# A second buffer for hT, finer waits of the gather, later constants and norm rows, and the wide expert one quad earlier

## What is computed

```python
def grouped_moe(x, router_w, router_b, w_gate, w_up, w_down):
    scores = jax.nn.sigmoid((t @ router_w).astype(jnp.float32))
    ...   # best of 4 groups, the top 2 experts in it, weights normalised
    for e in range(N_EXPERTS):                      # 16
        h = jax.nn.silu(t @ w_gate[e]) * (t @ w_up[e])      # 2048 -> 512
        y = y + combine[:, e:e + 1] * (h @ w_down[e])       # 512 -> 2048
    return y.reshape(B, S, D)
# in each layer
x = layer_norm(ALPHA * x + mix, ln_mix_g[i], ln_mix_b[i])
ffn = grouped_moe(x, ...)
x = layer_norm(ALPHA * x + ffn, ln_ffn_g[i], ln_ffn_b[i])
```

## Time and profile before

| | us |
|---|---|
| median of 3 runs (lowest, highest) | 1734.02 (1733.76, 1738.78) |
| the profiled execution's own time | 1737.14 |
| its span, first to last instruction | 1735.3 |
| mean granted clock of TensorE | 0.960 |

### The profile page before, as it was taken

The page is one execution under the profiler, slowest core; times in us unless marked ns, Lnnn a source line. Parts: engine busy times, 40 slices in busy tenths (PEclk is TensorE's granted clock), DMA queues, the critical chain, the costliest instruction groups (busy, mean ns, idle before and its releaser), DMA issues.

```text
span 1735.3 us, 19026 instructions
## 1 busy us (share of the span) xinstructions
PE 1585.9 (91%) x7841; PEld 934.2 (54%) x7841; DVE 668.1 (39%) x937; ACT 432.7 (25%) x551; POOL 29.4 (2%) x26
## 2 busy tenths in 40 slices
PE   6999999988989999999869999997999999999993
PEld 5888786875344343343338878785434334334331
DVE  4445335535123231323265474455232222222226
ACT  4334335324110111010135353333111110101112
POOL 1000000000000000000022000000000000000000
PEclk9999999997999999999979999898999999999997
DMA  9554323555999999999966565345799997998993
GB/s 364 205 194 191 122 97 128 212 182 207 420 427 414 428 427 428 428 428 428 428 261 251 189 224 182 131 165 224 282 428 428 427 428 308 422 375 361 429 427 142
DMA packets 47316, 531.18 MB, mean 306 GB/s; under 512 B 5361, under 2 KB 5905, under 8 KB 7938
## 3 DMA queue, kind: packets, MB, share of 16 engines
q1 hardware_dynamic: 45234, 518.08, 73.4%
q0 software_dynamic: 2000, 11.95, 1.9%
HBM read 527.91 MB, written 2.10 MB: 305 GB/s over the span
## 4 chain that ended last, share of the span: by engine, by line
PE 85%; DVE 6%; DMA 3%; ACT 3%; issue 1%; SPq 0%; POOL 0%; DVEq 0%; ACTq 0%
PE bank L1023 37%; PE bank L689 10%; PE bank L690 10%; PE bank L691 10%; PE bank L991 4%; PE bank L1072 4%; DMA w_all<-in_moe_w_down 3%; PE bank L1055 2%; PE bank L823 2%; ACT y_hi L1490 1%; PE bank L1002 1%; DVE X L2094 1%; PE bank L1110 1%; PE bank L896 1%; DMA w_land<-in_ev_w_in 1%
## 5 line engine op out<-in xcount | busy, mean ns | idle before, releaser
L1023 PE MATMUL bank<-w_all,xg 128*64 128x512 f32 x2048 | 454.5, 596 | 1.6 <-DVE hT L2074 1.4
L689 PE MATMUL bank<-w_hi,T_hi 128*128 128x512 f32 x768 | 303.1, 395 | 7.1 <-DVE w_lo L1650 4.6
L690 PE MATMUL bank<-w_lo,T_hi 128*128 128x512 f32 x768 | 301.0, 392 | 0.0
L691 PE MATMUL bank<-w_hi,T_lo 128*128 128x512 f32 x768 | 300.6, 391 | 0.0
L1650 DVE TENSOR_TENSOR w_lo<-w_land,w_hi 128x2048 fp32r<-128x2048 f32 (+1 forms) x96 | 214.2, 2240 | 210.7 <-ACT w_hi L1295 210.6
L1023 PEld LDWEIGHTS bank<-w_all,xg 128*64 128x64 f32 x2048 | 140.9, 137 | 278.3 <-issue 274.3
L1295 ACT CAST w_hi<-w_land 128x2048 fp32r<-128x2048 f32 (+1 forms) x100 | 184.3, 1854 | 247.9 <-PE bank L691 237.0
L1023 PE MATMUL bank<-w_all,hT 128*64 128x512 f32 x992 | 227.6, 602 | 2.2 <-DMA w_all<-in_moe_w_down 2.2
L2094 DVE SCALAR_TENSOR_TENSOR X<-bank,weight,X 128x512 f32<-128x512 f32 x256 | 174.4, 744 | 69.0 <-PE bank L1072 68.9
L2083 DVE TENSOR_TENSOR y_lo<-bank,y_hi 128x512 fp32r<-128x512 f32 x62 | 42.6, 688 | 387.3 <-ACT y_hi L1490 387.3
L689 PEld LDWEIGHTS bank<-w_hi,T_hi 128*128 128x128 f32 x768 | 145.4, 189 | 38.7 <-issue 3.1
(11 more groups left out here) (282 smaller groups left out, 1037.9 us busy)
## 6 DMA issues: line engine op xcount, KB each, us to landing
w_all<-in_moe_w_gate_up SPq DMA_DIRECT2D x128, 2048.0 KB, 15.1
w_all<-in_moe_w_down SPq DMA_DIRECT2D x64, 2048.0 KB, 18.9
w_land<-in_ev_w_in SPq DMA_DIRECT2D x32, 1024.0 KB, 4.8
w_land<-in_od_w_in SPq DMA_DIRECT2D x32, 1024.0 KB, 4.8
w_land<-in_ev_w_out SPq DMA_DIRECT2D x16, 1024.0 KB, 4.8
w_land<-in_od_w_out SPq DMA_DIRECT2D x16, 1024.0 KB, 4.8
w_land<-in_att_w SPq DMA_DIRECT2D x7, 1024.0 KB, 4.7
x0T<-in_xT SPq DMA_DIRECT2D x4, 512.0 KB, 9.7
```

Source lines behind the costliest of these rows:

```text
L689: pe.matmul(dst, hi_l, hi_r, start=start, stop=False)
L690: pe.matmul(dst, hi_l, lo_r, start=False, stop=False)
L691: return pe.matmul(dst, lo_l, hi_r, start=False, stop=stop)
L1023: ins = pe.matmul(dst[halves[h], :], cols(c), U.weights(q, pos + h)[:, c, :], start=start and c == 0, stop=stop and c == 3)
```

## The change

- hT has two buffers, hT_even and hT_odd, by the expert's number; product(e) waits only for the y_hi of expert e-2.
- The gather's wait for y_lo is taken apart: none before the first fill, half 0 before the second (bank 2), half 1 before the third (bank 3). The same holds in gather_wide.
- SP issues const behind the first twelve loads; PE waits for it behind block 1 and ACT before its sine tables. DVE's waits for const and for the small constants, ahead of its preparation of the sine tables, stay where they are.
- POOL issues the six small constants and the first norm rows only once PE has used 16 units, which is the end of block 3.
- In the last quad scatter(2, 1) is done between the two groups of the last down, and DVE does y_lo(3, 0) ahead of add(2, 1).
- WIDE_Q is 1: the wide expert stands at place 4, the fifth, and gather_wide serves the second quad.

```diff
@@ -50,7 +50,7 @@
 ROUNDS = SEQ // CAP
-WIDE_Q = 2
+WIDE_Q = 1
 WIDE = 4 * WIDE_Q
@@ -331,7 +331,8 @@
         gsil = moe_buf("gsil", [P, 4, ALL])
-        hT = moe_buf("hT", [P, 4, ALL])
+        hT_even, hT_odd = moe_buf("hT_even", [P, 4, ALL]), moe_buf("hT_odd", [P, 4, CAP])
+        hT = (hT_even, hT_odd)
         xg_x = moe_buf("xg_x", [P, KT, MORE])
@@ -510,8 +511,6 @@
         def _(sp):
-            sp.dma_start(const[:], A["const"]).then_inc(ident_in, 16)
-
             def load(g, j, src, n=NB, ring=w_land):
@@ -521,6 +520,7 @@
                 load(1, j, unit(w_in0, 0, j))
+            sp.dma_start(const[:], A["const"]).then_inc(ident_in, 16)
             with sp.Fori(1, IN0_FULL // 2) as i:
@@ -635,6 +635,33 @@
         def _(pool):
+            def load_rows(g, b, n):
+
+                if n:
+                    pool.wait_ge(rows_used, n)
+                pool.dma_start(rows[:, 0, :], g.partition_broadcast(P)).then_inc(rows_in, 16)
+                pool.dma_start(rows[:, 1, :], b.partition_broadcast(P)).then_inc(rows_in, 16)
...
+            pool.wait_ge(t_low, 8)
+            pool.wait_ge(used, 16)
             for dst, src in ((rw[:], A["router_w"]),
...
                 pool.dma_start(dst, src, allow_slow_non_contiguous=True).then_inc(const_in, 16)
-
-            def load_rows(g, b, n):
...
-            pool.wait_ge(t_low, 8)
             load_rows(A["ln_mix_g"][0:1], A["ln_mix_b"][0:1], 0)
@@ -734,7 +734,6 @@
-            pe.wait_ge(ident_in, 16)
             for j in range(4):
@@ -745,6 +744,7 @@
+            pe.wait_ge(ident_in, 16)
             pe.wait_ge(gemm_out_a, 1)
@@ -978,9 +978,12 @@
-            def gather(Q, n, qs=range(8)):
+            def gather(Q, n, qs=range(8), down_rows=None):
+
...
                 for q in qs:
+                    if q in (1, 2) and down_rows is not None:
+                        pe.wait_ge(y_lo_done, down_rows + q - 1)
                     if q >= 3:
@@ -992,9 +995,11 @@
-            def gather_wide(Q):
+            def gather_wide(Q, down_rows):
...
                 for t in range(KT):
+                    if t in (1, 2):
+                        pe.wait_ge(y_lo_done, down_rows + t - 1)
                     if t >= 3:
@@ -1087,16 +1092,18 @@
-                    def down(pos, e, following):
+                    def down(pos, e, following, between=None):
...
                             ge(pe, y_lo_done, 2 * E + (0 if is_wide(layer, q, e - 1) else p - 1))
-                            two_units(pos + 2 * p, bank[2 + p], lambda c: hT[:, c, 0:CAP], True, True)
+                            two_units(pos + 2 * p, bank[2 + p], lambda c: hT[e % 2][:, c, 0:CAP], True, True)
                             if p == 0 and following is not None:
...
                                 slots(following)
+                            if p == 0 and between:
+                                between()
@@ -1107,7 +1114,7 @@
                                 for c in range(4):
-                                    ins = pe.matmul(bank[2 + h][0:ALL, :], hT[:, c, :], U.weights(q, pos + 2 * p + h)[:, c, :],
+                                    ins = pe.matmul(bank[2 + h][0:ALL, :], hT_even[:, c, :], U.weights(q, pos + 2 * p + h)[:, c, :],
                                                     start=c == 0, stop=c == 3)
@@ -1148,16 +1155,14 @@
                         pe.wait_ge(slots_out, 4 * Q + 4)
-                        pe.wait_ge(y_lo_done, 2 * (4 * Q + 2) + 2)
                         if is_wide(layer, q, 4):
                             pe.wait_ge(twice_ready, Q + 2)
-                            gather_wide(Q + 1)
+                            gather_wide(Q + 1, 2 * (4 * Q + 2) + 1)
                         else:
-                            gather(Q + 1, 4)
+                            gather(Q + 1, 4, down_rows=2 * (4 * Q + 2) + 1)
                     first_sums(2, 3)
                     if last:
-                        scatter(2, 1)
-                        down(48, 3, None)
+                        down(48, 3, None, lambda: scatter(2, 1))
                         first_sums(3, None)
...
@@ -1323,7 +1328,6 @@
-            act.wait_ge(ident_in, 16)
             for j in range(4):
@@ -1349,6 +1353,7 @@
                                    accum_out=att[:, 2 * w + a:2 * w + a + 1]).then_inc(rms_sq, 1)
+            act.wait_ge(ident_in, 16)
             act.wait_ge(trig_ready, 1)
@@ -2070,11 +2075,11 @@
                         dve.wait_ge(silu_done, E + 1)
-                        ge(dve, y_hi_done, 2 * E)
-                        ins = dve.tensor_tensor(hT[:, :, 0:CAP], gsil[:, :, 0:CAP],
+                        ge(dve, y_hi_done, 2 * (E - 1))
+                        ins = dve.tensor_tensor(hT[e % 2][:, :, 0:CAP], gsil[:, :, 0:CAP],
                                                 bank[7][:, 0:4 * CAP].rearrange("p (c s) -> p c s", c=4), ALU.mult)
                         if is_wide(layer, q, e):
-                            ins = dve.tensor_tensor(hT[:, :, CAP:ALL], gsil[:, :, CAP:ALL], bank[6][:, 4 * CAP:8 * CAP]
+                            ins = dve.tensor_tensor(hT_even[:, :, CAP:ALL], gsil[:, :, CAP:ALL], bank[6][:, 4 * CAP:8 * CAP]
                                                     .rearrange("p (c s) -> p c s", c=4)[:, :, MORE:2 * MORE], ALU.mult)
@@ -2138,8 +2143,9 @@
                     if last:
+                        y_out(3, 0)
                         add(2, 1)
-                        down(3, None)
+                        y_out(3, 1)
                         add(3, 0)
...
```

More of the change, by code:

```diff
@@ L637, in _ @@
         def _(pool):
[L638 to L644, removed]
             def load_rows(g, b, n):
@@ L671, in _ @@
             pool.wait_ge(t_low, 8)
+            pool.wait_ge(used, 16)
+            for dst, src in ((rw[:], A["router_w"]),
+                             (rbias[:], A["router_b"].rearrange("(o e) -> o e", o=1).partition_broadcast(P)),
+                             (gains[:, 0, :], A["ev_q_norm"][0].rearrange("(t p) -> p t", t=4)),
+                             (gains[:, 1, :], A["ev_kv_norm"][0].rearrange("(t p) -> p t", t=4)),
+                             (gnorm[:], A["ev_gla_norm"].partition_broadcast(P)),
+                             (posi[:], pos_v)):
+                pool.dma_start(dst, src, allow_slow_non_contiguous=True).then_inc(const_in, 16)
             load_rows(A["ln_mix_g"][0:1], A["ln_mix_b"][0:1], 0)
@@ L1212, in overflow @@
                         for p in range(2):
-                            two_units(4 + p, bank[2], lambda c: hT[:, c, 0:CAP], True, True)
+                            two_units(4 + p, bank[2], lambda c: hT_even[:, c, 0:CAP], True, True)
                             after(V_, OVER_DVE, ("y", p))
@@ L2168, in overflow @@
                         after(A_, OVER_ACT, "silu")
-                        dve.tensor_tensor(hT[:, :, 0:CAP], gsil[:, :, 0:CAP],
+                        dve.tensor_tensor(hT_even[:, :, 0:CAP], gsil[:, :, 0:CAP],
                                           bank[7][:, 0:4 * CAP].rearrange("p (c s) -> p c s", c=4), ALU.mult) \
```

## The result

| us | before | after |
|---|---|---|
| median (lowest to highest), 4 runs each | 1736.4 (1733.8 to 1740.3) | 1712.8 (1712.1 to 1715.6) |
| the profiled execution's span | 1735.3 | 1711.0 |
| mean granted clock of TensorE | 0.960 | 0.972 |
| start to the first expert group | 417.5 | 413.4 |
| first layer's experts, first group to end of last down group | 460.9 | 457.8 |

The ratio after to before is 0.9874, 95% interval 0.9852 to 0.9897. The median lies 2.6 us under the 1715.4 foretold, inside the forecast's own range. Before's four runs lie high: in the 15, 23 and 7 runs beside the experiments its median is 1734.3, 1734.0 and 1733.5, so the change is worth about 21 us rather than 23.6. The span is 24.3 us shorter: 4.1 in the start, 3.1 in the first layer's experts, 2.3 between, 14.7 in the second layer's.

What follows compares the result with a forecast made beforehand. It took PE and the expert weight stream to be balanced in the MoE stages, PE-bound elsewhere. Start 5.2, first layer -1.4, second layer 14.8 sum to 18.6 us off: 1715.4 us, own range 1711 to 1719.

Steps and rivals of the forecast that it cites:

- What bounds it: MoE stages: PE and the weight stream balanced, 29.1 against 29.5 us an expert; PE waits for weights from mid first layer.
- hT: Product before each scatter: second buffer saves PE 1.21 us an expert, 27.3 us in 22 waits; expert 24.8 us for 26.0.
- Gather: PE's wait for y_lo before a gather goes to nothing: 3.4 us plus 1.7 of low clock, about 5.1 a boundary.
- First layer: First layer's MoE stage: a loss of 1.4 us (bounds: gain 5.1 without the sharing, loss 2).
- They now share with loads 94 and 95: End of first MoE stage: norm rows, started about 2 us after issue, split engines with the last loads, costing 4.9 us.
- so I charge the low clock: Last down group of first layer: PE has idled about 4 us, so 1.7 us is added.
- Second layer: Second layer's MoE stage: a gain of 14.8 us (bounds 20.5 without sharing, 11 with a slower stream).
- rival 2: Start gives only 2 and second layer's stream loses 4 us more in hiccups: gain 11.4, 1722.5 us; chance 0.12.
- The move is almost free either way: Wide expert at fifth or ninth place in second layer: load 95 lands within 1 us either way.
- Start: Before the first full block: 2.96 small constants, 1.4 const, 0.8 spared low clock; 5.2 us (bounds 2.0 and 6.5).
- Rival 4: Weight-bound loads, about 58: new weight waits keep PE's clock low, 2.0 us each, 1831 us; chance 0.03.
- Rival 1: Ends of both MoE stages: norm rows don't delay the last loads; 31 us off, 1703 us; chance 0.15.

Runs made afterwards that it cites:

- experiment 1: Kernel before, with each pair load behind the first six of each MoE stage cut to 3072 of 4096 columns, overflow rounds never entered: 1730.0 us (0.9979).
- 2: Changed kernel, with each pair load behind the first six of each MoE stage cut to 3072 of 4096 columns, overflow rounds never entered: 1658.7 us (0.9562).
- 7: Changed kernel, with an expert's product waiting again for both y_hi copies of the expert before, as if hT were single: 1722.0 us (0.9932).
- 4: Changed kernel, with GpSimd issuing each MoE stage's norm rows only once PE has used load 94: 1707.6 us (0.9849).
- 9: Changed kernel, with PE waiting again for y_lo of both halves before the whole gather, also the wide one: 1715.8 us (0.9902).
- 3: Changed kernel, with the second layer's wide expert at the ninth place again (WIDE_Q = 2): 1711.6 us (0.9875).
- 8: Changed kernel, with norm rows issued after load 94 was used and the wide expert at the ninth place: 1706.5 us (0.9837).
- 5: Kernel before, with only GpSimd's small constants and first norm rows waiting for used 16, const still ahead of xT: 1732.4 us (0.9987).
- 6: Kernel before, with only const moved behind block 1's loads and PE's and ACT's waits for it moved along: 1734.2 us (0.9997).
- experiment 10: Changed kernel, with scatter(2, 1) ahead of the last expert's two down groups again: 1717.8 us (0.9912).

## Why the prediction was right, and where its steps were not

A number in brackets is that of an experiment.

- **What bounds it: right.** PE-bound before (experiment 1), balanced so closely that the stream took most of what PE gave (2). PE's first wait of some length for weights stands at load 34 of the first layer, a third into the stage and not in its middle:

```profile
565.85 1.51 PE L1028 MATMUL bank<-w_all,xg 128*64 128x512 f32 x6 [0.98 <-DMA w_all<-in_moe_w_gate_up]
```

- **hT: right.** 24.70 us an expert for 24.8 (2), the waits ahead of scatter gone, and its worth in the time 9 us for 27 of waits, or 12.6 once the rows are moved away (7, 4). The product behind the wide expert still makes PE wait for 1.40 us.
- **Gather: right in sum, wrong in the split.** The wait fell to nothing, but the finer waits by themselves carry 1 to 3 us of it (9); the early product carries the rest. The prediction had said so in a half sentence and still counted the 5.1 as one step.
- **First layer: wrong, -1.4 foretold, +3.1 found.** Two terms were mis-sized. "They now share with loads 94 and 95": the issue fell at 856.2, the packets flowed only from 860 (3.7 us behind it, where the prediction had about 2), so only load 95 paid, 2.5 us for the 4.9. And "so I charge the low clock": behind 2.59 us without matmuls the last group took 3.65 and the clock fell only at 876; 1.7 was charged for nothing. 2.4 and 1.7 are 4.1 of the 4.5 between foretold and found.
- **Second layer: 14.8 foretold, 14.7 found, with errors that cancel; that the sum came out is partly luck.** Load 40 was issued 185.1 us after the stage's first group, where the steps gave 1405.7 - 1221.9 = 183.8 (the clock was low for 6.9 us in the wide down groups, 1378.4 to 1385.3, where before had 3.4). From its landing (1404.9) to load 95's (1680.4) 275.5 us passed, 2.5 of them for the rows: 4.96 a load for 4.91, hence 2.9 us of hiccups more, rival 2's mechanism in part. Against these and the 1.3 stand 2.2 of the rows and 1.7 of the clock, as in the first layer.
- **"The move is almost free either way": nearly.** It costs 1.2 us by the medians and 3 by the stages (3, 8), where I had written within 1.
- **Start: 5.2 foretold, 3.8 to 4.1 found in the traces.** The medians of the two halves show less, 1.6 and nothing (5, 6), so the size is open. GpSimd's transfers 3.5 for 2.96, const 0.3 for 1.4, and the 0.8 of spared low clock did not come: the idle time ahead of the full block stayed (2.47 for 2.60).
- **Between the layers, a term I did not have: 2.3.** It is no effect of the change. The stretch of low clock near 1090 us differs from trace to trace. These windows are of before and of after, at the same place of the work:

```profile
1085.00:1102.00 17.00, 13.29 (x49) 10.59 (x48) 9.07 (x14) 5.02 (x7) 0.00 (x0) 0.70 0.21 80
```

```profile
1078.00:1095.00 17.00, 13.25 (x59) 10.56 (x58) 8.99 (x14) 4.92 (x7) 0.00 (x0) 0.90 0.21 79
```

Experiment 1, with the old program there, shows 341.0 us for this part, as after does, and experiment 6, with the old program too, 343.5.
- **Rival 4 (a low clock in the weight waits): out.** In 740 to 850 us, where PE waits 1.2 to 1.5 us for three loads in six, the granted clock is 1.00. The Trainium skill, "TensorE: Matmul & The Clock Gate", section "HAM oscillation — how this bites in real kernels", tells of longer waits for weights that lower the clock anew each time; waits as long as those did not arise here. Rival 1 was half true, as the rows cost 2.5.

## What to carry to other kernels

Where an engine and a stream are within some per cent of each other, a saving on the engine is worth what the stream's end allows, not the sum of its waits: work out the stream's last landing first (here 96 loads of 4.9 us and its pauses) and then look at what delays that landing. Making the stream light for one run, with a quarter of each load left out, shows what the engine alone would take. What another queue issues within the last loads can delay the last of them (2.5 us for 2 MB of rows here), and it is the cheapest thing to move: one wait, about 5 us in the two layers. A saving on one engine can also bring such an issue forward, as the early product did.

## What was not expected of the hardware

- GpSimd's transfers of 1 MB each began 3.7 us behind their issue beside a full queue of SP (0.02 MB moved from 856.2 to 860) and 1.2 to 1.3 us behind it where that queue ran empty; then, beside the one load, they took 44% of the engines.
- The clock stayed at 2.4 GHz behind 2.59 us without matmuls (867.5 us of after), and fell in a stretch of 3.01 us of them (experiment 10), and before it had fallen behind 2.51. The length of the last idle stretch alone does not tell which.
- A stage with the same program differs by 2 to 4 us between the traces of two kernels, as the stretches of low clock in it differ (341.0 and 343.5 between the layers, 3.4 and 10.3 us of low clock near 1090 us; 411.4 to 415.3 for the start). That is as large as several effects measured here. Where the landings of the loads show the effect as well, as for the norm rows, it stands; where only a stage or only a median moves, it is open.
